# A layer norm between a projection and a convolution unit: ACT takes the root, sums and spreads move, activation tables are loaded elsewhere

## What is computed

```
x = _layer_norm(DEEPNORM_ALPHA * x + gate1 * y, ln1_g, ln1_b)     # y = merged @ w_out
h = x * (1.0 + scale2) + shift2
u = h @ w_up                                                      # w_up: 1024 x 5632
u = conv(u, conv_w, width 3, per channel) + conv_b
gate, val = split(u, 2)
y = (silu(gate) * val) @ w_down
```

## Time and profile before

| | us |
|---|---|
| median of 3 runs | 1793.59 (1792.66 to 1794.24) |
| the profiled execution's own time | 1791.98 |
| its span, first to last instruction | 1790.1 |
| matmuls of TensorE | 1753.5 busy, 98% of the span |
| VectorE, ScalarE, GpSimd | 970.8 (54%), 679.0 (38%), 825.7 (46%) |
| mean granted clock of TensorE | 0.996 |

### The profile page before, as it was taken

How to read it: one execution, slowest core, us unless ns; L and a number is a source line. 1 busy time by engine, 2 the same in 40 slices (tenths; PEclk the granted TensorE clock), 3 DMA queues, 4 the chain that set the end, 5 groups by cost and what they waited for, 6 DMA issues and landing times. The chain is left out here.

```text
span 1790.1 us, 26132 instructions
## 1 busy us (share of the span) xinstructions
PE 1753.5 (98%) x8971; PEld 1490.0 (83%) x8971; DVE 970.8 (54%) x1590; ACT 679.0 (38%) x1401; POOL 825.7 (46%) x664
## 2 busy tenths in 40 slices
PE   7999999999989999999999999999999999999997
PEld 6888888888777888888888888899988878888886
DVE  4257545767865467252124449476567673551544
ACT  4321222343476433222223223665532552332333
POOL 3554454568971445544444545201034465444551
PEclk9999999999999999999999999999999999999999
DMA  6454442534211345433323433100012134333321
GB/s 205 122 172 153 141 142 83 182 95 124 71 48 48 119 141 188 142 93 97 121 85 91 114 91 101 48 2 25 1 56 86 48 100 135 95 94 106 94 82 48
DMA packets 279699, 178.48 MB, mean 100 GB/s; under 512 B 6264, under 2 KB 258356, under 8 KB 279476
## 3 DMA queue, kind: packets, MB, share of 16 engines
q1 hardware_dynamic: 265348, 149.35, 28.8%
q10 hardware_dynamic: 14256, 27.87, 4.5%
HBM read 175.11 MB, written 2.10 MB: 99 GB/s over the span
## 5 line engine op out<-in xcount | busy, mean ns | idle before, releaser
L647 POOL TENSOR_TENSOR wL<-raw,wH 128x512 fp32r<-128x512 f32 (+2 forms) x560 | 748.1, 1359 | 897.9 <-ACT wH L1403 816.7
L753 PE MATMUL ps<-actH,wH 128*128 128x512 f32 (+1 forms) x1312 | 512.5, 391 | 6.8 <-DVE actL L2346 2.8
L753 PE MATMUL ps<-actH,wL 128*128 128x512 f32 (+1 forms) x1312 | 506.1, 386 | 0.0
L753 PE MATMUL ps<-actL,wH 128*128 128x512 f32 (+1 forms) x1312 | 506.0, 386 | 0.0
L1403 ACT ACTIVATE wH<-raw 128x512 fp32r<-128x512 f32 (+2 forms) x560 | 312.8, 608 | 337.4 <-PE ps L753 335.8
L753 PEld LDWEIGHTS ps<-actH,wH 128*128 128x128 f32 x1312 | 248.3, 189 | 57.3 <-issue 4.5
L753 PEld LDWEIGHTS ps<-actL,wH 128*128 128x128 f32 x1312 | 248.5, 189 | 48.9 <-issue 0.7
L753 PEld LDWEIGHTS ps<-actH,wL 128*128 128x128 f32 x1312 | 248.1, 189 | 49.1
L753 PE MATMUL ps<-hidH,wH 128*128 128x512 f32 (+1 forms) x720 | 268.1, 372 | 0.0
L753 PE MATMUL ps<-hidH,wL 128*128 128x512 f32 (+1 forms) x720 | 267.0, 371 | 0.0
L753 PE MATMUL ps<-hidL,wH 128*128 128x512 f32 (+1 forms) x720 | 266.9, 371 | 0.0
(11 more groups left out here) (339 smaller groups left out, 2079.0 us busy)
## 6 DMA issues: line engine op xcount, KB each, us to landing
mod_raw<-in_w_mod ACTq DMA_DIRECT2D x24, 1024.0 KB, 6.4
raw<-in_w_in SPq DMA_DIRECT2D x48, 512.0 KB, 3.7
raw<-in_ffn_w_gate SPq DMA_DIRECT2D x44, 512.0 KB, 3.9
raw<-in_ffn_w_up SPq DMA_DIRECT2D x44, 512.0 KB, 3.8
raw<-in_w_up SPq DMA_DIRECT2D x44, 512.0 KB, 3.8
raw<-in_ffn_w_down SPq DMA_DIRECT2D x32, 512.0 KB, 3.9
raw<-in_w_out SPq DMA_DIRECT2D x16, 512.0 KB, 3.7
raw<-in_w_down SPq DMA_DIRECT2D x16, 512.0 KB, 3.6
```

The costliest lines, as they stand in the source:

```text
L647: nc.gpsimd.tensor_tensor(wL[:, b:b + w // 2], raw[:, b:b + w // 2], wH[:, b:b + w // 2].bitcast(F32), ALU.subtract).then_inc(lo_ready, 1)
L753: return nc.tensor.matmul(out, a, b, start=first, stop=last)
```

## The change

Five things are done, all between `out2` and the first drain of `f3_up0`:

1. The three Newton steps of `rsqrt` for this norm are replaced: VectorE writes the variance, ACT takes `Sqrt` of it (`moment_root`), VectorE takes the reciprocal and does one Newton step (`moment_scale`).
2. TensorE's `spread_moments(0)` moves from the end of slab 2 of `out2`'s half 1 to behind its second tile.
3. `moments(1)` and `spread_moments(1)` move within half 0 of `third_slabs`: from behind tile 4 of slabs 0 to 2 and tile 1 of slab 3, to behind tiles 4 and 7 of slab 3.
4. VectorE's and ACT's programs of that stretch are put in another order: `normal(3)` to `normal(7)` stand earlier against the sums of half 1, and `affine(0)` to `affine(3)` earlier against ACT's splits and squares.
5. Two one-element activations are added, whose use is the table: `Sqrt` behind the late gate's `Sigmoid` before `merge`, `Silu` behind the second `moment_root`.

```diff
@@ third_slabs (TensorE)
-                        if (half, js, k) == (0, (0, 1, 2), 4):
+                        if (half, js, k) == (0, (3,), 4):
                             moments(1)
-                        if (half, js, k) == (0, (3,), 1):
+                        if (half, js, k) == (0, (3,), 7):
                             spread_moments(1)
@@ token_halves("out2", ...) (TensorE)
-                     lambda half, j, k: None if k < KT - 1 or half == 0 else
-                     moments(0) if j == 0 else spread_moments(0) if j == 2 else None)
+                     lambda half, j, k: moments(0) if (half, j, k) == (1, 0, KT - 1) else
+                     spread_moments(0) if (half, j, k) == (1, 2, 1) else None)
@@ ACT, before merge
         nc.scalar.activation(tile(gates, 15), tile(gates, 15), ACT.Sigmoid).then_inc(late_gate, 1)
+        nc.scalar.activation(exp_of_zero[:], zero[:], ACT.Sqrt).then_inc(table_set, 1)
         slabs("merge", 0, nothing)
@@ ACT, the norm
+        def moment_root(half):
+            act.wait_ge(ln_var, half + 1)
+            nc.scalar.activation(small[:, 16 + 2 * half:18 + 2 * half], small[:, 2 * half:2 * half + 2],
+                                 ACT.Sqrt).then_inc(ln_root, 1)
+
         split(third, 0, 0)
+        moment_root(0)
+        square(8)
         split(third, 0, 1)
-        square(8)
         square(9)
-        split(third, 0, 2)
         affine(0)
         affine(1)
+        split(third, 0, 2)
         square(10)
+        affine(2)
+        affine(3)
         split(third, 0, 3)
-        affine(2)
         square(11)
-        for n in range(3, 2 * KT):
+        for n in range(4, KT):
+            affine(n)
+        moment_root(1)
+        nc.scalar.activation(exp_of_zero[:], zero[:], ACT.Silu).then_inc(table_set, 1)
+        for n in range(KT, 2 * KT):
             affine(n)
@@ moments (VectorE)
-            link(V.scalar_tensor_tensor(small[:, two], ps[:, 5, 4 + 2 * half:6 + 2 * half], LN_EPS, md[:, two],
-                                        ALU.add, ALU.subtract))
-            rsqrt(rn[:, two], small[:, two], 2, last=(rn_ready, 4 + half), room=bank(5, 2, 20))
+            V.scalar_tensor_tensor(small[:, two], ps[:, 5, 4 + 2 * half:6 + 2 * half], LN_EPS, md[:, two],
+                                   ALU.add, ALU.subtract).then_inc(ln_var, 1)
+            dve.wait_ge(ln_var, half + 1)
+
+        def moment_scale(half):
+            two = slice(2 * half, 2 * half + 2)
+            y, v, a = bank(5, 2, 20), small[:, two], small[:, 64:66]
+            dve.wait_ge(ln_root, half + 1)
+            link(V.reciprocal(y, small[:, 16 + 2 * half:18 + 2 * half]))
+            link(V.tensor_tensor(a, v, y, ALU.mult))
+            link(V.scalar_tensor_tensor(a, a, -0.5, y, ALU.mult, ALU.mult))
+            V.scalar_tensor_tensor(rn[:, two], a, 1.5, y, ALU.add, ALU.mult).then_inc(rn_ready, 1)
+            dve.wait_ge(rn_ready, 4 + half)
@@ VectorE, the norm
         moments(0)
         second_tile(1, 0)
         centre(8)
+        moment_scale(0)
         second_tile(1, 1)
         centre(9)
         dve.wait_ge(row_bcast, 4)
...
         normal(2)
         add_square(9)
         low(1)
+        normal(3)
         second_tile(1, 3)
         centre(11)
-        normal(3)
         low(2)
+        normal(4)
         add_half(1, 0)
+        low(3)
+        normal(5)
         add_half(1, 1)
-        normal(4)
-        low(3)
         add_square(10)
+        normal(6)
         add_half(1, 2)
-        normal(5)
+        add_square(11)
+        normal(7)
         add_half(1, 3)
-        add_square(11)
-        normal(6)
-        normal(7)
         moments(1)
+        moment_scale(1)
         dve.wait_ge(row_bcast, 5)
```

More of the change, by code:

```diff
@@ L403, in _build @@
         "fin_T", "fin_sum", "fin_mean", "fin_sq", "fin_copy"))
+    ln_var, ln_root, table_set = sem("ln_var"), sem("ln_root"), sem("table_set")
     fin_var, fin_root, fin_gained = sem("fin_var"), sem("fin_root"), sem("fin_gained")
```

## The result

The changed kernel takes 1797.22 us (median of 9 runs, 1796.11 to 1799.15), the kernel before beside it on the same chip 1793.31 us (9 runs, 1790.43 to 1794.60). The ratio is 1.0022, interval 1.0014 to 1.0030: slower by 3.9 us (interval 2.5 to 5.4), where +4.1 was forecast. The profiled execution took 1798.13 us.

What follows compares the result with a forecast made beforehand. TensorE, busy 98% of the span, was taken as the bound. A second half starting 3.5 us later, 1.9 of low clock and -1.28 for the table load gave +4.1 us, 1797.7 on the median; range 1796.2 to 1799.3.

Steps and rivals of the forecast that it cites:

- First norm half: Shorter root and earlier spread, up to the first `normal` on VectorE: it starts 1.4 us earlier, at 1396.35.
- Tiles: First half's tiles on VectorE: port waits of 3.8 us put the eighth `normal` at 1411.95, nearly all the gain handed back.
- whole-operation price: Port waits in the first half's tiles: each held operation loses a whole GpSimd operation, 1.48 us, four 5.9.
- the row's own excess: Port waits in the first half's tiles: four VectorE operations held by at most 0.96 us each give 3.8.
- Second moments and spread: TensorE's end of the first half: sums at 1417.8, spread at 1420.9, second half starts 3.5 us later.
- H: Start of the second token half's first matmul on TensorE: 1421.46 before, forecast 1424.99.
- Clock: TensorE's gap before the second half: clock falls to 1.2 GHz for 6.8 us, costing 1.9 us, within 0 to 2.9.
- The rival that the clock holds: Clock stays up through the gap before the second half: +2.2 us, 1795.8; chance 0.13.
- Tables: First convolution drain on ACT: the table load of 1.28 us leaves the path, -1.28 us.
- `Identity`: Rival: ACT still loads tables for `Identity` in the convolution loop: +5.4 us, 1799.0; chance 0.07.
- Sum: Whole kernel: +3.5 + 1.9 - 1.28 = +4.1 us, 1797.7 on the median; chance 0.60.
- The rival of fewer port waits: First half's tiles meet no port waits: -2.4 us, 1791.2 with clock held, -0.5 with it fallen; chance 0.14.

Runs made afterwards that it cites:

- experiment 8: experiment 6 with VectorE's normals put beside GpSimd's pairs and the last four adds behind `normal(7)`: 1788.40 us against 1793.59 for the kernel before.
- experiment 3: Changed kernel with only TensorE's second moments and spread put back to their old places: 1795.97 us, ratio 1.0012 to the kernel before.
- experiment 6: Changed kernel with second moments behind tile 5 of slabs 0 to 2, spread behind tile 0 of slab 3: 1790.76 us against 1793.59 before.
- experiment 5: Changed kernel with 26 matmuls, results unread, added behind the second spread: 1795.79 us, ratio 1.0011 to the kernel before.
- experiment 1: Kernel before with only a one-element Silu added between `affine(7)` and `affine(8)`: 1791.97 us against 1793.81.
- experiment 4: Changed kernel without the one-element Silu activation: 1798.98 us, ratio 1.0030 to the kernel before.
- experiment 9: Changed kernel with only VectorE's order taken from experiment 8, moments and spread staying where the change put them: 1793.51 us against 1793.21 before.
- (7): Changed kernel with ACT's splits of slabs 2 and 3 each two `affine` earlier: 1798.00 us, ratio 1.0025 to the kernel before.
- 2: Kernel before with only TensorE's second moments and spread moved behind tiles 4 and 7 of slab 3: 1801.10 us, ratio 1.0038.

## Why the prediction was right

It held, and so did each of its steps. They are read from the profile with the 1.66 us shift taken off; N0 and N7 are the starts of the first and the eighth `normal`, M and R those of the second sums and the second spread:

- **First norm half.** N0 1396.30, forecast 1396.35; the second centre took 1.39 us beside GpSimd, so the port and not the root set it. Against the first sums N0 came 1.43 us earlier, forecast 1.4.
- **Tiles.** N7 1411.91, forecast 1411.95. The four held operations cost 0.74 + 0.95 + 0.98 + 0.95 = 3.62 us, and the fifth 0.24, forecast 3.8. By the whole-operation price that the prediction took from the Trainium skill's SBUF — State Buffer, "SBUF: two separate sides", it would have been 5.9; the row's own excess was the better term. That rule's mechanism, the later operation blocks until the earlier is through, agrees with this trace: each held operation ends 0.2 to 0.3 us behind one of GpSimd's, of which a pair is two at 1.35 us. `normal` and `second_tile`, which read one tensor in PSUM, took 0.41 to 0.48 us beside the same pairs, and experiment 8 lives on that.
- **Second moments and spread.** M to R took 3.14 us, forecast 3.1; the wait for `rn` was 1.01, forecast 1.2. R to H took 4.20, forecast 4.09, with 3.04 of waiting. H came 3.69 us later than before, forecast 3.5. M came at 1417.81 and R at 1420.95, forecast 1417.8 and 1420.9. With nothing but the two positions put back (experiment 3) the stretch is 3.65 shorter, and with the best two places that were tried 6.55 (experiment 6), clock included.
- **Clock.** Forecast 1.9 within 0 to 2.9; experiment 5 measured 2.23. The way of reckoning was right to the length of the low stretch, 6.8 us; only the part of it behind H was a guess, 4.4 us by the 1.9 where 5.2 was measured. The rival that the clock holds is out.
- **Tables.** Forecast -1.28; experiments 1 and 4 measured -1.25 and -1.33. `Identity` didn't bring a load back, so that rival is out too. The loads of that loop behind the first went too, and none had been in the path. Of the Sqrt load, which stands ahead of `out2`, TensorE saw nothing: ACT still idled 1.10 us before its next split, instead of 2.63. The Trainium skill, ScalarE: Activation LUTs, "What ACT_TABLE_LOAD costs", puts about 1.38 us of drain beside each load; by that page the gain would have been an estimated 2.66 us. No row here shows one, neither behind 4.55 us of idleness (experiment 4) nor right behind work: the Silu load starts at 1421.72, where the root ends at 1421.70.
- **Sum.** 3.69 + 0.99 (clock loss less table, 14.85 - 13.86) = 4.68 in the stretch, forecast 4.1; by the runs 3.9. H is 0.2 over its forecast and the clock 0.3. That 3.9 and 4.1 lie so close is partly luck: the interval of the runs is 2.5 to 5.4, and H can differ by some 0.6 us between executions (experiment 1). The prediction took 0.2% for the least difference that can be told; the interval here, 0.14% to 0.30%, is narrower than that.

The rival of fewer port waits could be made, by another VectorE order (experiment 9), and came out at no difference by the runs. Its price was too good: -0.5 with the clock fallen, where the stretch is 1.14 longer than before. N7 came 6 us earlier, earlier than the rival asked for, but the sums start 8.1 us behind it, not the 5.8 that the prediction counts. TensorE has no wait in the 6.3 us before them: with the tiles this early it is its own matmuls that set M, and that limit the rival had left out.

What I misjudged in the experiments was the old place of the sums under the new VectorE order (experiment 3): the wait there was foreseen, the fall of the clock behind it was not, and H gained 1.4 us instead of 3.1. That moving GpSimd's pairs alone would not free VectorE's list was expected, and came so (7). No run has the new root, or the new order of VectorE and ACT, as its only difference to the kernel before.

## What to carry to other kernels

A short chain of small operations (sums, root, spread) belongs under tiles that are ready; put behind the last of them its waits are bare (1.01 and 3.04 us here), and the clock that falls in the gap is charged on top. Its earliest place is set by the engine that makes its operands, so each time that engine's list is reordered the place has to be found again, and one tile decides between a wait of 2.36 us and none (experiments 3 and 6). Lay operations that read PSUM beside GpSimd's long ones, and keep those on two SBUF tensors for the time in between.

## What was not expected of the hardware

- In a gap of TensorE with two waits of 1.01 and 3.04 us and eight small matmuls between them the clock fell to 0.50; with 26 matmuls in it whose results are unread it stayed at 1.00, and the stretch was 2.23 us shorter. The price follows from where the low stretch of 6.8 us lies: only the part behind the gap, on matmuls that are ready, costs anything.
- The clock also fell where nothing had been changed: in the first block's attention (520 to 540 us) it is 0.83 in the changed kernel's profile and in those of experiments 1, 2 and 5, 0.91 in those of 4, 6, 7, 8 and 9, and 1.00 in that of before and of 3. Over the eleven kernels the norm's first sums start anywhere from 1388.82 (9) to 1392.24 (2), so a stretch is better compared than a span, and a single stretch still carries the 0.6 us of experiment 1.
- A GpSimd pair took 2.69 us beside VectorE's two-SBUF operations (2.96 in the kernel before) and 2.52 us beside normals: both sides pay for the meeting.
